# High and low parts of the split weights stored in pairs: TensorE's stationary operand read with a step of two

## What is computed

```python
proj  = h @ w_in                        # 2048 x 5456
mixed = cat(diff_out, dsa_out) @ w_o    # 2048 x 2048
ff    = (silu(h @ w_gate) * (h @ w_up)) @ w_down      # 2048 x 5632, twice, and 5632 x 2048
# second block: w_in_2 2048 x 3904, w_q_up_2, w_kv_up_2, w_out_2, w_gate_2, w_up_2, w_down_2
```

## Time and profile before

| what | value |
|---|---|
| median of 3 executions | 2602.88 us (2599.05 to 2606.17) |
| profiled execution, span from first to last instruction | 2602.4 us |
| mean granted TensorE clock | 0.984 of full speed |
| TensorE busy, matmuls / weight loads | 96% / 91% |
| VectorE, ScalarE, GpSimd busy | 55%, 40%, 11% |
| matmuls of L2108, L2109, L2110 | 3 x (4608 + 1408) = 18,048 of 20,022 |
| units split (L933, L1456) | 386 |

### The profile page before, as it was taken

The page is one execution under the profiler, slowest core; times in us unless marked ns, Lnnn a source line. Parts: engine busy times, 40 slices in busy tenths (PEclk is TensorE's granted clock), DMA queues, the critical chain, the costliest instruction groups (busy, mean ns, idle before and its releaser), DMA issues.

```text
span 2602.4 us, 47889 instructions
## 1 busy us (share of the span) xinstructions
PE 2494.1 (96%) x20022; PEld 2363.1 (91%) x20022; DVE 1441.4 (55%) x1926; ACT 1033.4 (40%) x1332; POOL 292.1 (11%) x372
## 2 busy tenths in 40 slices
PE   6999988989999999999989998998999999999999
PEld 4999847969999999999979997778999999999999
DVE  3677657965674444433455555655655555554443
ACT  3533244344333343333334336443444444443333
POOL 5000122410100000011113002113000000000000
PEclk8999989989999999999989999999999999999999
DMA  9887864977786555555544442313455555555553
GB/s 343 288 285 269 288 210 171 333 270 236 246 289 198 179 186 184 176 180 186 179 137 154 141 152 65 125 65 130 146 179 188 181 177 180 179 189 178 179 180 127
DMA packets 263862, 504.24 MB, mean 194 GB/s; under 512 B 17152, under 2 KB 26283, under 8 KB 263467
## 3 DMA queue, kind: packets, MB, share of 16 engines
q1 hardware_dynamic: 257899, 494.97, 56.9%
q10 hardware_dynamic: 5840, 7.52, 0.9%
HBM read 498.04 MB, written 2.10 MB: 192 GB/s over the span
## 4 chain that ended last, share of the span: by engine, by line
PE 78%; DVE 8%; ACT 4%; issue 4%; DMA 3%; SPq 1%; ACTq 1%; POOL 1%; DVEq 0%; POOLq 0%
PE bank L2108 24%; PE bank L2110 23%; PE bank L2109 23%; ACT w_hi L933 3%; DVE w_lo L1456 3%; PE bank L2143 1%; DMA raw<-in_w_in 1%; DVE ada_acc L1484 1%; DVE tmp L1590 1%; DMA staged<-in_w_ada 1%; SPq L644 1%; PE bank L2252 1%; SPq L737 1%; PE bank L2453 0%; ACTq L1065 0%
## 5 line engine op out<-in xcount | busy, mean ns | idle before, releaser
L1456 DVE TENSOR_TENSOR w_lo<-raw,w_hi 128x2048 fp32r<-128x2048 f32 (+3 forms) x386 | 862.9, 2236 | 954.0 <-ACT w_hi L933 953.6
L2108 PE MATMUL bank<-x_hi,w_hi 128*128 128x256 f32 (+2 forms) x4608 | 1320.8, 287 | 33.7 <-DVE w_lo L1456 19.1
L2109 PE MATMUL bank<-x_lo,w_hi 128*128 128x256 f32 (+2 forms) x4608 | 1308.3, 284 | 0.0
L2110 PE MATMUL bank<-x_hi,w_lo 128*128 128x256 f32 (+2 forms) x4608 | 1307.7, 284 | 0.0
L933 ACT ACTIVATE w_hi<-raw 128x2048 fp32r<-128x2048 f32 (+3 forms) x386 | 718.9, 1862 | 1043.6 <-PE bank L2110 916.5
L2108 PEld LDWEIGHTS bank<-x_hi,w_hi 128*128 128x128 f32 x4608 | 874.2, 190 | 70.0 <-issue 39.7
L2110 PEld LDWEIGHTS bank<-x_hi,w_lo 128*128 128x128 f32 x4608 | 876.1, 190 | 0.0
L2109 PEld LDWEIGHTS bank<-x_lo,w_hi 128*128 128x128 f32 x4608 | 872.3, 189 | 1.2 <-issue 1.2
L2108 PE MATMUL bank<-hid_hi,w_hi 128*128 128x256 f32 x1408 | 399.6, 284 | 2.2 <-DVE x_res L2004 1.1
L2110 PE MATMUL bank<-hid_hi,w_lo 128*128 128x256 f32 x1408 | 398.4, 283 | 0.0
L2109 PE MATMUL bank<-hid_lo,w_hi 128*128 128x256 f32 x1408 | 398.4, 283 | 0.0
(11 more groups left out here) (332 smaller groups left out, 1458.4 us busy)
## 6 DMA issues: line engine op xcount, KB each, us to landing
raw<-in_w_gate SPq DMA_DIRECT2D x88, 1024.0 KB, 5.2
raw<-in_w_up SPq DMA_DIRECT2D x88, 1024.0 KB, 5.2
raw<-in_w_ada SPq DMA_DIRECT2D x72, 1024.0 KB, 6.6
raw<-in_w_in SPq DMA_DIRECT2D x68, 1024.0 KB, 5.7
raw<-in_w_down SPq DMA_DIRECT2D x64, 1024.0 KB, 5.0
raw<-in_w_down SPq DMA_DIRECT2D x32, 768.0 KB, 4.3
beside<-in_w_ada SPq DMA_DIRECT2D x16, 1024.0 KB, 7.7
raw<-in_w_o SPq DMA_DIRECT2D x16, 1024.0 KB, 6.3
```

The lines of the kernel that those rows point to most:

```text
L1456: dve.tensor_tensor(w_lo[ps][:, 0:width], raw[slot][:, 0:width], w_hi[ps][:, 0:width], ALU.subtract).then_inc(raw_free[slot], 1)
L2108: pe.matmul(out, wh[:, k, c], hi(k0 + k), start=a0, stop=False)
L2109: pe.matmul(out, wh[:, k, c], lo(k0 + k), start=False, stop=False)
L2110: ins = pe.matmul(out, wl_[:, k, c], hi(k0 + k), start=False, stop=z)
```

## The change

The four split tiles become two, `w_both0` and `w_both1`, each 128 partitions by 2048 by 2. `w_hi` and `w_lo` are views of them: element i of the high part stands at position 2i and element i of the low part at 2i + 1, so the two parts of one weight lie in the same eight bytes. The bytes taken are the same and they lie in the same stretch of SBUF, so no other tile moves. All reads and writes of either part (L933, L979, L1456, L2091 with L2108 to L2110) now have a step of two elements, eight bytes. No instruction, wait, DMA or buffer is added or taken away.

```diff
         raw = [place(f"raw{i}", [P, UK * COLS]) for i in range(RAW)]
-        w_hi = [place(f"w_hi{i}", [P, UK * COLS], F32R) for i in range(SPLIT)]
-        w_lo = [place(f"w_lo{i}", [P, UK * COLS], F32R) for i in range(SPLIT)]
+        w_both = [place(f"w_both{i}", [P, UK * COLS, 2], F32R) for i in range(SPLIT)]
+        w_hi, w_lo = ([w[:, :, part] for w in w_both] for part in range(2))
         x_res = place("x_res", [P, KT, N2])
```

## The result

| | before | after |
|---|---|---|
| median, us (lowest to highest), 4 executions each | 2604.48 (2599.05 to 2606.17) | 2626.46 (2623.17 to 2630.78) |
| ratio to before, 95% interval | | 1.0093 (1.0076 to 1.011) |
| profiled execution's span, us | 2602.4 | 2624.2 |
| TensorE busy, matmuls / loads, us | 2494.1 / 2363.1 | 2514.5 / 2384.4 |
| ScalarE / VectorE busy, us | 1033.4 / 1441.4 | 1099.7 / 1438.4 |

A forecast was written before the change was run, and what follows sets the result against it. TensorE was taken as the bound, with matmuls filling 96% of the span. The terms summed as 2602.4 + 0 + 0 = 2602.4 us for the span, 2603 us for the median, range 2594 to 2665 us.

The forecast's parts named there:

- The bound: Whole kernel: TensorE bounds it, matmuls filling 96% of the span and weight loads 91%.
- Rival B: Dense matmuls: the load's wider reach slows the moving side, 4.4 ns each, 79 us, so 2682 us; chance 0.10.
- Rival C: L933 and L1456: stepped writes lengthen the splits; 18% on both gives 28 us, 2630 us; chance 0.07.
- Stationary reads: L2108 to L2110, 18,048 loads with a step of two: 0 ns each, 0 us.
- 6.9 ns to spare under each matmul: Dense matmuls: a 128-column load takes 111.4 ns under a matmul of 118.3 ns.
- L933 and L1456: The two splits, 386 units, stepped writes and one stepped read: 0 added, bounds nothing and twice as long.
- the steady cover: Steady units: both splits together may grow by 1.44 us before TensorE waits.
- The doubling of both splits: L933 and L1456 doubled: 8.4 us per unit against 5.68, 1070 us more, so 3670 us.
- Addresses, DMAs, L979: Nothing behind the tiles moves, DMAs never touch them; L979 at the start, doubled, under 4 us.
- Rival A: Every dense matmul: load needs a second fetch per column pair, pace 227 ns, 1949 us, so 4550 us; chance 0.06.
- Rival D: Dense matmuls: faster if the new layout stops operands getting in each other's way, up to 125 us, 2478 us; chance 0.05.
- The forecast marks: Profile after: matmul starts 118 to 120 ns apart, loads 190 to 192 ns, L933 1915 and L1456 2302 ns.

The follow-up runs named there:

- pe_stepped: Changed kernel with only TensorE's loads at a step of two, ScalarE and VectorE contiguous: 2614.83 us against 2601.10 for the kernel before, ratio 1.0059.
- writers_stepped: Changed kernel with only ScalarE and VectorE at a step of two, TensorE's loads contiguous: 2612.68 us against 2601.10 for the kernel before, ratio 1.0035.
- paces: Bare matmul streams from one filled tile, model's work left out; pitch of x, 256 columns: rows 118.3, pairs 119.6, blocks 117.4 ns per matmul.

## Why the prediction was right or wrong

**The bound** was read rightly: what moved the time is TensorE's pace on the three dense lines, and ScalarE's and VectorE's parts matter only where the chain passes them. One reading was off by little: the first of the 14 matmuls of the earlier trace rows starts 0.11 us before VectorE ends, and only the other 13 see neither engine at work.

**The range** of 2594 to 2665 us holds the result, but the sum, 2603 us, missed it by 23 us, and the range reached that far only for Rivals B and C. Neither came as described, so that it held is in part luck.

**Stationary reads, "I take 0 ns"**: this step failed, and with it the forecast of no change. Its argument was that the moving side already goes through 1024 bytes in 118 ns. The load's own read at step 2 costs 117.8 ns and not 111.7, and the 0 should have been about 1 ns on the mean of 18,048 matmuls (18.3 us by the paces, 0.59% or about 15 us by `pe_stepped`). The bounds were no cost and a load of 227 ns; 117.8 lies near the lower one, but not on it. (227 is the load of the earlier trace rows at the lower granted clock; twice 111.4 is 223, and the load that takes twice as long, at step 4, took 233.) Behind it stands a second error: "6.9 ns to spare under each matmul" took the pace for the larger of two independent times, so that a load longer by 6.1 ns would stay hidden. The pace at 256 columns is no such constant. It moves between 113 and 122 ns with the distance of the operands' starts, and with a stepped load none of the fixed pairs tried came below 120. In the trace of before this could be seen: the earlier trace rows had 118.3 ns and the earlier trace rows 120.0 for the same shape, and the text used both without asking why. "TensorE: Matmul & The Clock Gate" of the Trainium skill, section "Step-by-step: what each phase is for", has two independent read ports; here the pace moves from 113.2 to 120.0 ns by the start of one operand alone, so if there are two ports, the reads behind them aren't independent in time.

**L933 and L1456, "the pace of one element at a time, so there is no packing that a step would break"**: right for L1456 (2302 to 2301 ns), wrong for L933 (1915 to 2096). The bounds and the place were right: the steady cover shrank by 0.1 us and held, and only the units on the chain pay. With the prediction's own rule, L933's 3% of the chain, 78 us, grow by 9.5% to give 7.4 us; `writers_stepped` measured 0.35%, 9.1 us (5 to 13). (The doubling of both splits, 386 x 2.8, is 1081 us and not 1070; nothing hangs on it.)

**Addresses, DMAs, L979** at nothing: no run separates them. The two halves together give the whole loss, but with intervals of 0.14 to 0.17% on each of the three ratios, some 7 us either way could hide here.

**Rival A** (a second fetch per pair): no; that is what step 4 does, at 233 ns. **Rival B** had the right place, the pace, with 121 to 124 ns where 119.7 came. Its cause, that the wider reach slows the moving side, is at best half of it: the load itself is longer, 117.8 in place of 111.7 ns with hardly a moving side there, and at steps 3 and 4 its length alone is the pace under 256 columns (173.3 and 233.5 ns). At step 2 and 256 columns no run separates length from reach, since a step changes both. Its 2.2 ns for 64 columns came from 12 and 13 matmuls; over all starts of the trace it is 126.0 against 125.1, 0.9 ns. **Rival C** was half the truth: 9.5% on one of the two lines in place of 18% on both. The loss is B's place and C's together, which the prediction had only one by one; both lay in the range. **Rival D**: pairs gave no gain, but its reason, that the operands get into each other's way by where they lie, was real, and a shift of 192 bytes brings 27 of the 125 us it allowed for.

**The forecast marks** were too coarse: "118 to 120 ns apart" would have passed for no change, while the 1.5 ns between 118.2 and 119.7, over 9120 matmuls, are 13.8 us. Loads of 190 to 192 ns in the records were the mark that spoke at once, with 199 on `x`.

## What to carry to other kernels

Where a kernel is bound by thousands of short matmuls, a load that seems to have room can still cost: price it per matmul, and compare the pace of equal shapes in different stages before calling any difference noise. Keep a stationary operand at a step of one, and at most two; where high and low parts have to lie together, put them in blocks, not in pairs (blocks were tried in bare streams only, at 117.4 ns against 119.6). And try the start addresses of both operands in the kernel itself, because the same distance gave 113.3 or 117.8 ns in different streams, and a shift of 192 bytes was worth 1.1% here, about as much as the change under study cost.

## What the runs showed of the hardware

- Weight load of 128 x 128 four-byte elements, full granted clock: 111.7, 117.8, 173.3, 233.4 ns at steps 1 to 4. At half the clock: 213 ns at steps 1 to 3, still 233 at step 4.
- Matmul of 256 columns with such a load: 113.2 to 120 ns by the distance of the two starts modulo 256 bytes, slow at 0, quick at 64, 112 and 192 bytes; at 64 and 192 it was 117.7 to 117.8 in other streams. With a load of step 2 and fixed starts, 120.0 to 121.1 at every distance tried.
- ScalarE writing 2048 elements: 1909, 2035, 2905, 3808 ns at steps 1 to 4. VectorE's subtraction: 2292 and 2294 at steps 1 and 2, 2904 and 3790 at 3 and 4.
- With 272 columns, where the moving side is longer than any load tried in the kernels, pairs are 0.5 ns quicker than rows (126.0 to 125.5, in the kernels and in `paces`); no run says why.
